# Router products of tile 1 moved ahead of the place counts, and expert 0's rows gathered already transposed

## The chip, the cores and the metric

The kernel runs on one core of a Trainium2 chip. The metric is the device time of one execution in microseconds; lower is better. The engines that matter here are TensorE (PE for its matrix products, PEld for its loads of stationary operands), VectorE (DVE), ScalarE (ACT) and the queue of weight transfers, which SyncE (SP) issues.

## What is computed

One transformer layer on 256 tokens of width 1024, in float32: attention of two kinds (MoBA and NSA, 8 heads each), the output projection with its residual, and a mixture of 32 experts with 4 picked for each token. The part around the change is the beginning of the mixture. Cut from the reference:

```python
x = x + jnp.concatenate([o_moba, o_nsa], axis=-1) @ w_out[l]
x = x + moe_ffn(rmsnorm(x, ffn_norm_g[l]), w_router[l], b_router[l], w_up[l], b_up[l], w_down[l], b_down[l])

# moe_ffn(h):
logits = (ht @ w_router + b_router).astype(jnp.float32)
top_val, top_idx = lax.top_k(logits, TOP_K)          # 4 of 32 experts for each token
wts = jax.nn.softmax(top_val, axis=-1)
# for each expert, with the rows of the tokens that picked it:
a = clamped_swiglu(xb @ w_up[e] + b_up[e])           # 1024 -> 2048 -> 1024
y = a @ w_down[e] + b_down[e]                        # 1024 -> 1024
# and the sum over a token's four experts, weighted by wts
```

The weights of one expert are 12 MB (w_up 8 MB, w_down 4 MB), so 32 experts bring some 400 MB through the transfer queue.

## The kernel before

The 256 tokens are two tiles (0 and 1) of 128 tokens, one token on each partition: `xt[:, n, :]` holds tile n with its 1024 columns. After attention the kernel does the following, in program order on TensorE (lines 1282 to 1315).

- **Projection and turned tiles.** `project` (L1028) multiplies the attention output by w_out, VectorE adds the residual into `xt` (`add_piece`, L1573), and `turn_x2` transposes 128x128 blocks of `xt` (L914) into PSUM, from where ScalarE copies them to `x2T` (`read_x2T`, L789). Tile 1 is turned in three steps: blocks 0 to 3, blocks 4 and 5, blocks 6 and 7.
- **Router.** `route` (L1108) sums eight products of a block of `x2T` (stationary, 128x128) with 32 router columns. Each float32 product shows as two loads and two products in the trace; a transpose shows as one.
- **Top 4.** `top_of(n)` on VectorE (L1579 to L1585) adds the bias, finds the four largest logits of each token of tile n and marks them in `M[:, n, :]`. L1297, L1298 and L1308 are products of a triangle and of ones with `M`, which count the tokens ahead, so that `place_of` (L1591) knows each token's place in each expert's list. `pick_tile(n)` (L1595) makes `pm[:, n, :]`, 128 tokens by 64 places, with the token's 1/rms where it takes that place.
- **Gather of an expert.** `gather_tile(n)` (L1118) multiplies `pm[:, n, :]` (stationary, 128x64) by the 1024 columns of `xt` in two halves of 512, into bank XG of PSUM, and sums over the two tiles. The result lies as places by columns, so ScalarE copies it to `xg` (`read_xg`, L815), `gather_turn` transposes it in four blocks (L1133) into bank XTB, and VectorE multiplies it by the norm's gain into `xgT` (`read_xgT`, L1637). `xgT[:, k, :]` is the stationary operand of the up products.
- **Up, down, combine.** `up` (L1163, 64 loads and 64 products an expert, over blocks k = 0 to 7), preceded by the bias product `up_bias` (L1143); `down` (L1196); `combine` (L1208). `keep_warm` (L1114) issues products whose result nobody reads.
- **Expert 0** has this order of its own: tile 0's `gather_tile` before the counts of tile 1, tile 1's after them, then the bias, the transposes, three warm products, and `up`. ScalarE, between its last copy of `x2T` and `read_xg(0)`, takes the exponential of the top logits (L809) and loads the table for its sigmoid (L810).

The order on every engine is written out by hand; there is no scheduler. The weights arrive in `ring`, ten places of 2 MB, plus `extra`; SyncE issues each transfer when the place has been used. Right around the change it waits first for `logits_done` 2 (the end of tile 1's router products), then for `first_half_used` 1 and 2 (the up products of expert 0 at k = 0 and k = 2), then for `up_used` and `down_used` of the experts that follow.

## Time and profile before

| | |
|---|---|
| median of 3 runs | 1076.32 us |
| lowest and highest of them | 1074.85 and 1077.40 us |
| the profiled execution: its time | 1077.45 us |
| the profiled execution: its span | 1075.4 us |
| mean granted TensorE clock | 0.995 of full |
| TensorE busy | 1031.2 us (96%) |
| VectorE, ScalarE busy | 223.5 us (21%), 155.0 us (14%) |
| transfers | 423.35 MB, mean 394 GB/s |

The span runs from the first to the last instruction of the core; 2.05 us of the profiled execution's time lie outside it. All times of the trace below are in microseconds from the start of the span. TensorE is shown as busy nearly always, but the transfer queue is too, and which of the two is waited for changes along the span, so the share of busy time alone does not tell what an edit is worth.

### The profile page before, as it was taken

Reading aid. Unit: us, or ns where it says so; the run is one execution under the profiler, and the core shown is the slowest. Engines: PE = TensorE matmul, PEld = TensorE weight load, DVE = VectorE, ACT = ScalarE, POOL = GpSimd, SP = SyncE. Lnnn points to the kernel's source line nnn. Section 1 sums busy time; section 2 is a strip of 40 time slices with the busy share of each in tenths; the row PEclk is TensorE's granted clock in tenths of the full one; section 3 lists DMA queues with packets and bytes.
Section 4 is the critical chain, followed back from the end, with each engine's and each line's share of the span. In section 5 each row is a group of like instructions: output and inputs, shape, how many; then the busy total and the mean of one; then the engine's idle time right before and its main releaser. Section 6 shows DMA issues by size and latency. Waiting matters only on the chain.

```text
span 1075.4 us, 12842 instructions
## 1 busy us (share of the span) xinstructions
PE 1031.2 (96%) x5122; PEld 411.5 (38%) x5122; DVE 223.5 (21%) x633; ACT 155.0 (14%) x389; POOL 20.0 (2%) x49
## 2 busy tenths in 40 slices
PE   8999999999999999999999999999999999999996
PEld 6776663333333333333333333333333333333332
DVE  3354533111111111111111111111112101111112
ACT  1233431111100110001111111111101100011102
POOL 4011000000000000000000000000000000000000
PEclk8999999999999999999999999999999999999999
DMA  9993378999999999999999999999999999999994
GB/s 283 317 351 129 121 288 356 403 399 428 427 428 431 433 432 433 431 428 430 431 431 433 435 431 430 430 431 431 436 429 433 430 429 427 427 427 427 428 425 193
DMA packets 36972, 423.35 MB, mean 394 GB/s; under 512 B 8242, under 2 KB 12386, under 8 KB 19012
## 3 DMA queue, kind: packets, MB, share of 16 engines
q1 hardware_dynamic: 36688, 422.34, 94.1%
q8 instruction: 32, 0.52, 0.2%
q10 hardware_dynamic: 244, 0.42, 0.1%
q14 instruction: 8, 0.07, 0.0%
HBM read 421.70 MB, written 1.05 MB: 393 GB/s over the span
## 4 chain that ended last, share of the span: by engine, by line
PE 77%; DMA 19%; DVE 3%; ACT 1%; issue 0%; DVEq 0%; ACTq 0%; SPq 0%
PE ps L1163 31%; DMA ring<-in_w_up_dram 18%; PE ps L1196 17%; PE ps L1208 5%; PE ps L1118 4%; PE ps L941 4%; PE ps L1028 3%; PE ps L948 2%; PE ps L1143 2%; PE ps L979 1%; DVE work L1637 1%; PE ps L1133 1%; DVE work L1681 1%; PE ps L1176 1%; PE ps L1055 1%; PE ps L1067 1%
## 5 line engine op out<-in xcount | busy, mean ns | idle before, releaser
L1163 PE MATMUL ps<-ring,work 128*64 128x512 f32 x2040 | 447.4, 594 | 8.6 <-DMA ring<-in_w_up_dram 8.1
L1163 PEld LDWEIGHTS ps<-ring,work 128*64 128x64 f32 x2040 | 142.7, 137 | 310.3 <-issue 290.7
L1196 PE MATMUL ps<-ring,work 128*64 128x512 f32 x1008 | 223.3, 595 | 21.1 <-DVE work L1681 21.1
L1646 DVE TENSOR_SCALAR work<-ps 128x512 f32<-128x512 f32 x31 | 21.4, 692 | 642.9 <-PE ps L1163 642.9
L1196 PEld LDWEIGHTS ps<-ring,work 128*64 128x64 f32 x1008 | 69.8, 137 | 154.5 <-issue 129.0
L821 ACT ACTIVATE work<-work 128x512 f32<-128x512 f32 x31 | 19.5, 630 | 453.8 <-DVE work L1646 453.8
L1208 PE MATMUL ps<-work 64*128 64x512 f32 x256 | 63.6, 615 | 0.7 <-ACT work L833 0.7
L1118 PE MATMUL ps<-xt,work 128*64 128x512 f32 x256 | 60.6, 593 | 0.2 <-DVE work L1595 0.2
L833 ACT ACTIVATE work<-ps 128x512 f32<-128x512 f32 x32 | 19.1, 597 | 236.5 <-PE ps L1196 236.5
L941 PE MATMUL ps<-extra,ring 128*128 128x256 f32 x192 | 42.7, 380 | 0.0
L1208 PEld LDWEIGHTS ps<-work 64*128 64x128 f32 x256 | 22.0, 186 | 41.8 <-issue 40.2
L941 PEld LDWEIGHTS ps<-extra,ring 128*128 128x128 f32 x192 | 35.9, 190 | 5.0 <-issue 0.4
L1143 PE MATMUL ps<-work 32*64 32x512 f32 x256 | 34.8, 613 | 0.5 <-ACT work L856 0.5
L1637 DVE TENSOR_TENSOR work<-ps,gf_rowsT 128x512 f32<-128x512 f32 x32 | 22.1, 692 | 54.3 <-PE ps L1133 54.3
L1118 PEld LDWEIGHTS ps<-xt,work 128*64 128x64 f32 x256 | 18.2, 137 | 35.8 <-issue 35.4
L1028 PE MATMUL ps<-ring,extra 128*128 128x512 f32 (+1 forms) x72 | 28.7, 546 | 0.0
L948 PE MATMUL ps<-ring,extra 128*128 128x280 f32 (+1 forms) x64 | 22.0, 497 | 0.0
L1649 DVE SCALAR_TENSOR_TENSOR work<-work 128x512 f32<-128x512 f32 x31 | 21.5, 692 | 1.1
L1653 DVE TENSOR_TENSOR work<-work 128x512 f32<-128x512 f32 x31 | 21.5, 692 | 1.1
L1647 DVE TENSOR_SCALAR work<-ps 128x512 f32<-128x512 f32 x31 | 21.1, 681 | 0.0
L815 ACT ACTIVATE work<-ps 128x512 f32<-128x512 f32 x32 | 19.1, 598 | 11.2 <-PE ps L1118 11.2
L828 ACT ACTIVATE work<-ps 128x256 f32<-128x256 f32 x32 | 12.4, 387 | 50.9 <-PE ps L1176 50.9
(254 smaller groups left out, 525.7 us busy)
## 6 DMA issues: line engine op xcount, KB each, us to landing
ring<-in_w_up_dram SPq DMA_DIRECT2D x40, 4096.0 KB, 35.8
ring<-in_w_up_dram SPq DMA_DIRECT2D x43, 2048.0 KB, 18.2
ring<-in_w_down_dram SPq DMA_DIRECT2D x20, 4096.0 KB, 35.9
ring<-in_w_down_dram SPq DMA_DIRECT2D x21, 2048.0 KB, 15.6
ring<-in_w_up_dram SPq DMA_DIRECT2D x9, 1024.0 KB, 13.6
ring<-in_w_in_dram SPq DMA_DIRECT2D x8, 1024.0 KB, 9.4
ring<-in_w_out_dram SPq DMA_DIRECT2D x4, 1024.0 KB, 9.7
ring<-in_w_down_dram SPq DMA_DIRECT2D x4, 1024.0 KB, 30.0
```

The source lines that it names most:

```text
L941: t = pe.matmul(dst, lhs(win_unit(c, k)), normed(k), start=(k == 0), stop=(k == KD - 1))
L948: t = pe.matmul(dst, normed(k)[:, n * P:(n + 1) * P], win_unit(c, k)[:, lo:hi], start=(k == 0), stop=(k == KD - 1))
L1028: t = pe.matmul(dst, oT[:, k, n * P:(n + 1) * P], wout_nsa[:, k, lo:hi] if k < 4 else wout_moba[:, lo // 512, k % 4, lo % 512:lo % 512 + h ...
L1118: t = pe.matmul(ps[h * 64:(h + 1) * 64, XG, :], pm[:, n, :], xt[:, n, h * 512:(h + 1) * 512], start=(n == 0), stop=(n == 1), skip_group_ch ...
L1143: t = pe.matmul(UP[h * 64:h * 64 + 64, a, :], sel[a * E:a * E + E], bup[a * E:a * E + E, :].rearrange("e (p h x) -> e p h x", h=2, x=8)[:, ...
L1163: t = pe.matmul(UP[h * 64:h * 64 + 64, a, :], xgT[:, k, :], row[:, a * 64:(a + 1) * 64, h, :], start=False, stop=(k == KD - 1), skip_group ...
L1196: t = pe.matmul(ps[h * 64:(h + 1) * 64, XG, :], aT[:, j, u * 64:u * 64 + 64], w[:, j * D + h * 512:j * D + (h + 1) * 512], start=(u == 0 a ...
L1208: t = pe.matmul(ps[:, OUT[n][h], :], cT[h * 64:(h + 1) * 64, n, :], yv[h * 64:(h + 1) * 64, :], start=first, stop=True, skip_group_check=True)
L1637: dve.tensor_tensor(xgT.rearrange("p (h j) t -> p j h t", h=2), ps[:, XTB, :].rearrange("p (j h t) -> p j h t", j=4, h=2), gf_rowsT[:].uns ...
L1646: dve.tensor_scalar(t1, up_pairs[:, 0], 7.0, None, ALU.min).then_inc(swi, 1)
L1649: dve.scalar_tensor_tensor(out=t3, in0=t3, scalar=1.0, in1=t1, op0=ALU.add, op1=ALU.mult)\
L1653: dve.tensor_tensor(av, t3, t2, ALU.mult).then_inc(a_ready, 1)
```

## The change

Three things are edited on the way from tile 1's router to expert 0's up products.

1. The first four of tile 1's eight router products are issued before the two count products of tile 0 and the transposes of blocks 6 and 7; before, all eight came behind them.
2. Expert 0's rows are gathered with the operands exchanged: blocks of `xt`, taken with a step of 4 columns, are the stationary operand (128x128), and `pm` (128x64) is the moving one. The result is already transposed, so ScalarE's copy `read_xg(0)` and the four transposes `gather_turn(0)` are gone. There are 16 such products, 8 for each tile. Those of tile 0 are issued behind the router products; those of tile 1 behind `pm_ready`. The halves of the result lie in banks XTB and XG, and VectorE reads each with an operation of its own (`read_first`).
3. `up` of expert 0 waits for the first half of `xgT` alone (`first_xgT`) and for the second only at k = 4. The bias product now stands ahead of the two warm products, the three other warm products are gone, and the later waits on `xg_read` count one less.

```diff
--- before.py
+++ after.py
@@ -315,6 +315,8 @@
         table_done = sem("table_done")
         first_half_used = sem("first_half_used")
         logits_done = sem("logits_done")
+        first_gathered = sem("first_gathered")
+        first_xgT = sem("first_xgT")
         td_ready = sem("td_ready")
         te_ready = sem("te_ready")
         x2T_ready = sem("x2T_ready")
@@ -838,7 +840,6 @@
                 act.activation(sel[0:2 * E], eye2[0:2 * E, ds(e, 1)].broadcast_to([2 * E, TOK]), ACT.Copy)\
                    .then_inc(sel_ready, 1)
 
-            read_xg(0)
             select(1, 1)
             sigmoid(0)
             read_xg(1)
@@ -1113,10 +1114,12 @@
                 for _ in range(n):
                     pe.matmul(ps[:, OUT[0][0], 0:P], ident[:, :], ones[:], start=True, stop=True)
 
-            def gather_tile(n):
-                for h in range(2):
-                    t = pe.matmul(ps[h * 64:(h + 1) * 64, XG, :], pm[:, n, :], xt[:, n, h * 512:(h + 1) * 512],
-                                  start=(n == 0), stop=(n == 1), skip_group_check=True)
+            def first_gather(n, half):
+
+                for j in range(4):
+                    t = pe.matmul(ps[:, (XTB, XG)[half], j * TOK:(j + 1) * TOK],
+                                  xt[:, n, 512 * half + j:512 * half + 512:4], pm[:, n, :],
+                                  start=(n == 0 and j == 0), stop=(n == 1), skip_group_check=True)
                 return t
 
             def gather(b, first=False):
@@ -1124,11 +1127,13 @@
                 if not first:
                     pe.wait_ge(y_read, b - 1)
                 for n in range(NT):
-                    t = gather_tile(n)
+                    for h in range(2):
+                        t = pe.matmul(ps[h * 64:(h + 1) * 64, XG, :], pm[:, n, :], xt[:, n, h * 512:(h + 1) * 512],
+                                      start=(n == 0), stop=(n == 1), skip_group_check=True)
                 t.then_inc(xg_done, 1)
 
             def gather_turn(b):
-                pe.wait_ge(xg_read, b + 1)
+                pe.wait_ge(xg_read, b)
                 for j in range(4):
                     t = pe.transpose(ps[:, XTB, j * P:(j + 1) * P], xg[:, j * P:(j + 1) * P], ident[:, :])
                 t.then_inc(xgT_done, 1)
@@ -1145,18 +1150,22 @@
                                       start=True, stop=False, skip_group_check=True)
                 t.then_inc(bias_used, 1)
 
-            def up(b, prev, unit, biased=False, last=False, halves=False):
-
-                if not biased:
+            def up(b, prev, unit, last=False, first=False):
+
+                if first:
+                    pe.wait_ge(first_xgT, 1)
+                else:
                     up_bias(b, prev)
-                pe.wait_ge(xgT_read, b + 1)
+                    pe.wait_ge(xgT_read, b + 1)
                 for u in range(UP_UNITS):
+                    if first and u == 2:
+                        pe.wait_ge(xgT_read, b + 1)
                     w = unit(u)
                     for j in range(2):
                         k = 2 * u + j
                         if last and k == KD - 1:
                             pe.wait_ge(last_half_in[u], 16)
-                        row = aside if halves and k == 1 else w[:, j * 2 * F:(j + 1) * 2 * F]
+                        row = aside if first and k == 1 else w[:, j * 2 * F:(j + 1) * 2 * F]
                         row = row.rearrange("k (p h x) -> k p h x", h=2, x=8)
                         for a in range(2):
                             for h in range(2):
@@ -1165,13 +1174,13 @@
                                               start=False, stop=(k == KD - 1), skip_group_check=True)
                             if last and k == KD - 1 and a == 0:
                                 t.then_inc(half_up, 1)
-                        if halves and k in (0, 2):
+                        if first and k in (0, 2):
                             t.then_inc(first_half_used, 1)
                     t.then_inc(up_used, 1)
 
             def combine_turn(b, ahead):
                 pe.wait_ge(pw_ready, b + 1)
-                pe.wait_ge(xg_read, b + 1 + ahead)
+                pe.wait_ge(xg_read, b + ahead)
                 for n in range(NT):
                     t = pe.transpose(ps[:, XG, n * P:(n + 1) * P], pw[:, n, :], ident[:, :])
                 t.then_inc(cT_done, 1)
@@ -1292,27 +1301,26 @@
             turn_x2(1, range(0, 4), PJ[0], 3, 1)
             project(ps[:, 6, 0:256], 1, 768, 1024, 4).then_inc(half_done, 1)
             turn_x2(1, range(4, 6), PJ[1], 4, 2)
+            route(1, range(0, 4), 3)
             pe.wait_ge(m_ready, 1)
             pe.wait_ge(const_ready, 7)
             pe.matmul(ps[:, PLACES[0], 0:E], upper[:], M[:, 0, :], start=True, stop=True).then_inc(pos_done, 1)
             pe.matmul(ps[:, PLACES[1], 0:E], ones[:], M[:, 0, :], start=True, stop=False)
             turn_x2(1, range(6, 8), PJ[0], 5, 3)
-            route(1, range(0, 4), 3)
             route(1, range(4, 6), 4)
             route(1, range(6, 8), 5).then_inc(logits_done, 1)
-            pe.wait_ge(bup_in, 32)
-
             pe.wait_ge(pm0_ready, 1)
-            gather_tile(0)
+            first_gather(0, 0)
+            first_gather(0, 1)
             pe.wait_ge(m_ready, 2)
             pe.matmul(ps[:, PLACES[1], 0:E], upper[:], M[:, 1, :], start=False, stop=True).then_inc(pos_done, 1)
+            pe.wait_ge(bup_in, 32)
+            up_bias(0, False)
             keep_warm(2)
             pe.wait_ge(pm_ready, 1)
-            gather_tile(1).then_inc(xg_done, 1)
-            up_bias(0, False)
-            gather_turn(0)
-            keep_warm(3)
-            up(0, False, in_singles(0), biased=True, halves=True)
+            first_gather(1, 0).then_inc(first_gathered, 1)
+            first_gather(1, 1).then_inc(xg_done, 1)
+            up(0, False, in_singles(0), first=True)
             gather(1, first=True)
             combine_turn(0, 1)
             gather_turn(1)
@@ -1632,8 +1640,15 @@
                     t = dve.tensor_scalar(pw[:, n, :], iota_t, place(n), Wt[:, n, ds(e, 1)], ALU.is_equal, ALU.mult)
                 t.then_inc(pw_ready, 1)
 
+            def read_first(half, done, ready):
+
+                dve.wait_ge(done, 1)
+                k = slice(4 * half, 4 * half + 4)
+                dve.tensor_tensor(xgT[:, k, :], ps[:, (XTB, XG)[half], 0:4 * TOK].rearrange("p (k t) -> p k t", k=4),
+                                  gf_rowsT[:, :, half:half + 1].broadcast_to([P, 4, TOK]), ALU.mult).then_inc(ready, 1)
+
             def read_xgT(b):
-                dve.wait_ge(xgT_done, b + 1)
+                dve.wait_ge(xgT_done, b)
                 dve.tensor_tensor(xgT.rearrange("p (h j) t -> p j h t", h=2),
                                   ps[:, XTB, :].rearrange("p (j h t) -> p j h t", j=4, h=2),
                                   gf_rowsT[:].unsqueeze(3).broadcast_to([P, 4, 2, 64]),
@@ -1681,7 +1696,8 @@
                 dve.tensor_copy(aT[:, 2:4, :], UP[:, 1, 0:256].rearrange("p (a q) -> p a q", a=2))\
                    .then_inc(aT_read, 1)
 
-            read_xgT(0)
+            read_first(0, first_gathered, first_xgT)
+            read_first(1, xg_done, xgT_read)
 
             dve.wait_ge(te_ready, 1)
             link(dve.tensor_tensor(texp, texp, M, ALU.mult))
```

On TensorE, from the transposes of blocks 4 and 5 of tile 1 to expert 0's first up products, the program before has these rows (each is line, kind, output<-moving operand,stationary operand, shape of the output, and count; `work` is the tensor in which `pm`, `M`, `xgT` and the router's columns lie, and `extra` holds `x2T`):

```order
L914 MATMUL ps<-ident,xt 128x128 x2
L1297 MATMUL ps<-work,upper 128x32
L1298 MATMUL ps<-work,ones 128x32
L914 MATMUL ps<-ident,xt 128x128 x2
L1108 MATMUL ps<-work,extra 128x32 x8
L1118 MATMUL ps<-xt,work 64x512 x2
L1308 MATMUL ps<-work,upper 128x32
L1114 MATMUL ps<-ones,ident 128x128 x2
L1118 MATMUL ps<-xt,work 64x512 x2
L1143 MATMUL ps<-work 64x512 x4
L1133 MATMUL ps<-ident,work 128x128 x4
L1114 MATMUL ps<-ones,ident 128x128 x3
L1163 MATMUL ps<-ring,work 64x512 x4
```

and the changed program has these (its line numbers are somewhat higher for the same statements; L1109 is `route`, L1120 the new gather, L1148 the bias, L1115 `keep_warm`, L1172 `up`):

```order
L915 MATMUL ps<-ident,xt 128x128 x2
L1109 MATMUL ps<-work,extra 128x32 x4
L1307 MATMUL ps<-work,upper 128x32
L1308 MATMUL ps<-work,ones 128x32
L915 MATMUL ps<-ident,xt 128x128 x2
L1109 MATMUL ps<-work,extra 128x32 x4
L1120 MATMUL ps<-work,xt 128x64 x8
L1316 MATMUL ps<-work,upper 128x32
L1148 MATMUL ps<-work 64x512 x4
L1115 MATMUL ps<-ones,ident 128x128 x2
L1120 MATMUL ps<-work,xt 128x64 x8
L1172 MATMUL ps<-ring,work 64x512 x4
```

Four router products moved ahead of the counts, the gather of 64x512 products became one of 128x64 products, and the four transposes L1133 and three warm products have no successor before `up`.

On VectorE, from tile 1's `pick_tile` to the sums of the softmax (the two rows between them are the difference of the logits and the read of the gathered rows), before:

```order
L1595 TENSOR_SCALAR work<-work,rstd 128x64
L1620 TENSOR_TENSOR work<-work 128x64
L1637 TENSOR_TENSOR work<-ps,gf_rowsT 128x4x2x64
L1687 TENSOR_TENSOR work<-work 128x64
L1688 TENSOR_REDUCE work<-work 128x2
```

and in the changed program, where L1647 is `read_first`:

```order
L1603 TENSOR_SCALAR work<-work,rstd 128x64
L1628 TENSOR_TENSOR work<-work 128x64
L1647 TENSOR_TENSOR work<-ps,gf_rowsT 128x256 x2
L1703 TENSOR_TENSOR work<-work 128x64
L1704 TENSOR_REDUCE work<-work 128x2
```

One read of 128x512 became two of 128x256; what is behind them stands as it did. On ScalarE only the copy L815 of expert 0 between the table load L810 and `select(1, 1)` (L838) is gone.

## Rows read from the trace of the kernel before

**Rows 1.** The page: TensorE and its share; the queue of the weights.
```profile
PE 1031.2 (96%) x5122; PEld 411.5 (38%) x5122; DVE 223.5 (21%) x633; ACT 155.0 (14%) x389; POOL 20.0 (2%) x49
...
q1 hardware_dynamic: 36688, 422.34, 94.1%
```

**Rows 2.** Chain of waits, 620 to 720 us: start, length, what.
```profile
634.02 37.00 DMA ring<-in_w_up_dram
...
691.04 38.26 DMA ring<-in_w_up_dram
```

**Rows 3.** Windows: PE, PEld, DVE, ACT, POOL busy, granted clock, DMA share, GB/s.
```profile
168.00:170.00 2.00, 2.00 (x12) 0.68 (x10) 1.20 (x6) 0.00 (x0) 0.00 (x0) 1.00 0.11 45
170.00:172.00 2.00, 2.00 (x12) 0.72 (x10) 0.00 (x0) 0.00 (x0) 0.00 (x0) 1.00 0.74 242
...
220.00:222.00 2.00, 2.00 (x16) 0.44 (x14) 0.00 (x0) 0.85 (x2) 0.00 (x0) 1.00 0.74 213
222.00:224.00 2.00, 2.00 (x12) 0.68 (x10) 0.00 (x0) 0.00 (x0) 0.00 (x0) 1.00 0.71 270
224.00:240.00 16.00, 16.00 (x79) 5.86 (x76) 2.76 (x5) 1.62 (x3) 0.00 (x0) 1.00 1.01 425
```

**Rows 4.** Timeline of SyncE's queue, 150 to 235 us: start, length, issues.
```profile
169.46 0.33 SPq L483 DMA_DIRECT2D ring<-in_w_down_dram  x1
172.89 2.04 SPq L483 DMA_DIRECT2D ring<-in_w_up_dram  x2
```

**Rows 5.** Chain of waits, 150 to 200 us.
```profile
159.43 1.72 PE ps L1108 x16
...
161.24 0.26 DVE work L1579
...
162.49 0.42 PE ps L1308 x2
...
163.25 0.32 DVE work L1595
...
164.00 1.28 ACT L810
165.29 0.20 ACT root L810
165.50 0.50 ACT work L815
...
166.04 0.67 PE ps L1133 x4
...
166.73 0.70 DVE work L1637
...
167.48 13.95 PE ps L1163 x64
...
192.99 1.02 PE ps L1143 x8
```

**Rows 6.** Timeline of TensorE, 158 to 163 us: start, length, operation.
```profile
158.42 0.30 PEld L1297 LDWEIGHTS ps<-work,upper 128*128 128x128 f32 x2
...
158.99 0.44 PE L914 MATMUL ps<-ident,xt 128*128 128x128 f32 x2
...
159.16 1.86 PEld L1108 LDWEIGHTS ps<-work,extra 128*128 128x128 f32 x16
...
161.06 0.20 PEld L1118 LDWEIGHTS ps<-xt,work 128*64 128x64 f32 x4
...
162.71 0.53 PEld L1114 LDWEIGHTS ps<-ones,ident 128*128 128x128 f32 x4
```

**Rows 7.** Timeline of VectorE and ScalarE, same stretch.
```profile
158.51 0.42 DVE L1573 TENSOR_TENSOR xt<-ps,xt 128x256 f32<-128x256 f32 x1 [0.92 <-PE ps L1028]
...
159.47 0.38 ACT L789 ACTIVATE extra<-ps 128x256 f32<-128x256 f32 x1 [0.35 <-PE ps L914]
```

**Rows 8.** Timeline of stationary loads near the start, two overlapping stretches.
```profile
8.18 0.55 PEld L928 LDWEIGHTS ps<-ident,ring 2*128 2x128 f32 x4
...
8.51 0.21 PEld L928 LDWEIGHTS ps<-ident,ring 2*128 2x128 f32 x1
```

## Prediction

> **What bounds the kernel now.** I read the page first. TensorE is busy for 96% of the span, and the weight queue takes 94% of the transfer engines' time [rows 1]. Two engines so near to full cannot be told apart by their shares, so the next view is the chain of waits. From 634 us on, its long pieces are transfers of w_up of 37 to 38 us [rows 2]: that stretch is bound by the weights, with TensorE's down, gather and up products between as the links that release the next transfer. So an edit near 160 us is worth what it does to the stream of weights, and nothing else.
>
> The windows say where that stream can still be moved. From 224 us on the share is 1.01 at 425 GB/s: it never pauses. Before, it does. Between 168 and 172 us it moves 45 and 242 GB/s, and between 220 and 224 us 213 and 270 GB/s [rows 3]. Against 425 the last pause is worth (1 - 213/425) x 2 + (1 - 270/425) x 2 = 1.7 us. The queue's timeline shows what ends the first: SyncE issues at 169.46 and 172.89 us [rows 4], when the up products of expert 0 have used blocks 0 and 2. So the pauses are waits for TensorE. If TensorE starts `up(0)` earlier by d and then does the same work, each release after it comes earlier by d, the pauses lie earlier, and so does the stream's unbroken part, whose last transfer decides the end. The transfers in flight before 168 us are not moved; the idle time behind them is more than (1 - 45/425) x 2 = 1.8 us [rows 3], so d may be that large before it is cut.
>
> **Where up(0) starts now.** The chain between the router and `up` [rows 5]: router products to 161.15, top 4 on VectorE from 161.24, the count product at 162.49, place and pick to 163.25 + 0.32 = 163.57. Then it turns to ScalarE: a table load of 1.28 us from 164.00 and a small operation at 165.29 stand ahead of the copy `read_xg(0)` (0.50 on the chain, to 166.00), and then come the transposes at 166.04, VectorE's read at 166.73 (0.70) and `up` at 167.48. The gather itself is not on it; it waited for ScalarE's table. The reader should see that all of 163.57 to 167.48, 3.9 us, is this detour.
>
> **The change, step by step.** I follow the time at which TensorE begins a load of stationary operands. The cadence of loads of 128 columns is that of the router: 16 in 1.72 us, 0.1075 us each [rows 5]. Both old and new orders are the same up to 158.42, where the first count product was loaded [rows 6].
>
> 1. *Router order.* Four router products, 8 loads: 0.86, to 159.28. Two count products: one took 0.22 (four loads of 0.1075 for both are 0.43), to 159.72. The transposes of blocks 6 and 7: their loads took 159.16 - 158.99 = 0.17, to 159.89, and their result was there 0.44 after the first load [rows 6], so at 160.16. ScalarE's copy takes 0.38 [rows 7] and starts 0.04 later, 160.58; with the gap of 0.04 to 0.06 that the chain shows between engines, block 6 is usable at 160.64. Meanwhile TensorE does blocks 4 and 5: 4 loads, to 160.32, and waits 0.32. This is a **new wait**: before, the four products now moved away lay between these transposes and the router products that need them. Last 4 loads to 161.07, where before 16 loads from 159.16 [rows 6] ended at 160.88. So logits come **0.19 later**. The stall of VectorE's residual add, which held the transposes at 158.99 (0.12 us beyond the 158.42 + 0.43 of the two products), is absorbed in this. Queued behind the new wait are the last router products and everything after; `logits_done` also releases one half transfer of w_down, but the queue then still has work to 168 us, so 0.19 is hidden there, and would cost 0.19 if it were not.
> 2. *Tile 0's gather.* Before, its first load came 0.18 after the router's last (161.06 against 160.88 [rows 6]); I keep that: 161.25. 8 products of 2 loads at 0.1075 are 1.72, to 162.97. The trace has no load of `xt` by steps of 4 over 128 partitions with 64 moving columns; the moving columns lie between the router's 32 and the transposes' 128, both of which run at about this cadence [rows 5, 6], so I take 0.1075. Under it VectorE's top 4 runs: its chain took 162.49 - 161.24 = 1.25 [rows 5], so from 161.43 the mask is there at 162.68. TensorE comes later, 162.97: the count product is now late because of TensorE, by 0.3.
> 3. *Count, bias, warm products.* Count 0.22 (162.49 to 162.71 [rows 6]), to 163.19. Bias 1.02 (the 8 of L1143 later in the chain [rows 5]), to 164.21. Two warm products, 4 loads, 0.43, to 164.64. VectorE needs from the count's load to the pick 163.57 - 162.49 = 1.08 [rows 5]: 162.97 + 1.08 = 164.05. So the pick is covered by bias and warm products with 0.6 to spare; without them it would cost up to 0.86.
> 4. *Tile 1's gather.* 16 loads, 1.72, to **166.36**. The first half's 8 loads end at 165.50; the last product ends 0.27 after the turn of its load (router: 161.15 against 160.88), so 165.77. VectorE reads 256 columns from PSUM in 0.42 [rows 7], with 0.04 on either side: 166.27. Just before 166.36, so `up` starts when TensorE is free. The second read needs to be done only at k = 4, and `up` takes 13.95 for eight blocks [rows 5], so 7.0 us later: free.
> 5. *Removed.* ScalarE's copy, four transposes and three warm products. ScalarE's exponential and table load are off the path now; `select(1, 1)` and the sigmoid need them only after `up(0)`.
>
> `up(0)` at 166.36 instead of 167.48: **1.1 us earlier**, less than the 1.8 that the first pause can give. Nothing after it is changed. For the profiled execution, 1077.45 us with a span of 1075.4, this gives 1076.3 and 1074.3; it was the slowest of the three, 1.1 above their median. On the median, 1076.32 - 1.1 = **1075.2**.
>
> **Bounds of the unknown price.** Below: if the 32 new loads cost nothing, the count goes out at 162.68, bias and warm products end at 162.68 + 0.22 + 1.02 + 0.43 = 164.35, and the path is then VectorE's, 164.35 + 0.27 + 0.04 + 0.42 + 0.04 = 165.12: gain 2.4. Half the price gives about 1.7. Above: each load longer by x costs 32x; the gain is gone at x = 0.035, a cadence of 0.1425. The nearest row for the step of 4 is L928, which loads `gf_rows` by the same step: 4 loads, the first at 8.18, the last at 8.51, so 0.11 us each [rows 8]. They hold 2 partitions only, but 128 columns as here; so I stay at 0.1075.
>
> The Trainium skill speaks against this change (SBUF — State Buffer, section on the DMA port swizzle): SBUF lines are 16 bytes, and full bandwidth wants at least two hits in a line, though the same passage calls a step of 4 floats free. By its first half every column of this gather opens a line of its own. L928's cadence of 0.11 does not show it; the sum with doubled loads is that of the second rival below.
>
> **Rivals.**
> - *The stream does not follow* (0.14): `up(0)` is earlier, but the end stays, 1076.3. For it: the end is set 900 us later, through transfers of 37 us, and the three runs spread over 2.5 us. Against it: the last pause ends by TensorE's release and is 1.7 us, more than the shift.
> - *Slow stepped loads* (0.08), the other side: each of the 32 loads takes twice as long, 32 x 0.1075 = 3.44 more, `up(0)` at 169.8, 2.3 later than before: 1078.6. It decides from a cadence of 0.1425 for a loss, and from 0.1425 + 2.15/32 = 0.21 for one beyond 0.2%. Against it: L928.
> - *Cheaper loads or better overlap* (0.06): half the price, 1.7 earlier, 1074.6. For it: 64 moving columns need less of the array than 128. Against it: the router's 32 need no less time.
>
> **How the numbers follow.** The forecast has 0.72: 0.8 to 1.3 us faster, since a cadence of 0.117 for 32 loads takes 0.3 back. The range: lowest run less 1.7, 1073.2; highest run with nothing gained, 1077.4, and a little of the slow loads, 1077.6. What a measurement of this kernel can tell from no change is about 0.2%, 2.15 us. The forecast is half of that. A median may be off by 1 us, so beyond 2.15 faster comes from the tail of the forecast and the third rival, 0.14; slower from the second and from spread, 0.06; within, 0.80.
>
> **What would show it.** Right: `up(0)` begins near 166.4 (it has to be within 166.1 to 166.7); a wait of about 0.3 us before the last four router loads, on ScalarE's copy; no wait before the count product of tile 1 nor before tile 1's gather; new loads at 0.11 us; issues of SyncE near 168.3 and 171.8; the last pause of the stream near 219 to 223. Wrong: loads above 0.14 us, a wait of `up` on VectorE of more than 0.2 us, the second half late at k = 4, or a pause of the stream that ends no earlier than before. If all of this holds and the time has moved by more than 2 us, the cause is not this edit's path.

## The result

The changed kernel takes 1082.06 us (median of 4 runs, 1080.59 to 1083.40) against 1075.59 us for the kernel before in the same comparison: ratio 1.0059, 95% interval [1.0047, 1.0071], some 6.3 us slower by the ratio (the two medians lie 6.5 apart). The forecast was 1075.2 us, faster by 1.1. The profiled execution took 1080.59 us, with a span of 1078.6 us.

Line numbers are those of the changed kernel: L1109 is `route`, L1120 the transposed gather, L1316 the count product, L1148 the bias, L1115 the warm products, L1172 `up`. The chain of waits of the changed kernel, 100 to 300 us (start, length, what), to be held against [rows 5]:

```profile
148.83 0.87 PE ps L915 x8
...
157.10 0.39 ACT extra L791
...
157.54 0.63 PE ps L1109 x4
158.17 3.81 PE ps L1120 x16
161.98 0.37 PE ps L1316 x2
162.35 1.91 PE ps L1148 x8
164.27 1.15 PE ps L1115 x4
165.42 3.60 PE ps L1120 x16
169.02 16.10 PE ps L1172 x64
...
197.70 13.88 PE ps L1172 x64
```

Two things are wrong against the forecast. Each gather of 16 loads takes 3.81 and 3.60 us where 1.72 was expected. And from the count product on, everything is slow that the change does not touch: the bias 1.91 instead of 1.02, `up(0)` 16.10 instead of 13.95 [rows 5]. The windows say why (columns as in [rows 3]; the granted clock is the number before the DMA share):

```profile
156.00:158.00 2.00, 1.89 (x18) 1.78 (x18) 1.10 (x6) 0.88 (x3) 0.00 (x0) 1.00 0.85 254
158.00:160.00 2.00, 2.00 (x11) 2.00 (x10) 1.05 (x6) 0.97 (x1) 0.00 (x0) 0.95 1.03 360
160.00:162.00 2.00, 2.00 (x11) 2.00 (x10) 0.00 (x0) 0.00 (x0) 0.00 (x0) 0.50 0.91 324
...
172.00:174.00 2.00, 2.00 (x8) 0.61 (x6) 0.00 (x0) 0.00 (x0) 0.00 (x0) 0.63 0.36 57
174.00:176.00 2.00, 2.00 (x12) 0.61 (x10) 0.00 (x0) 0.00 (x0) 0.00 (x0) 1.00 0.81 332
```

TensorE's clock falls from 2.4 to 1.2 GHz (granted 1.00 to 0.50) during the first transposed gather, with TensorE shown as busy for the full 2.00 us of each window from 158 us on, and comes back some 14 us later, inside `up(0)`. The slow loads are there before the clock falls. Timeline of the stationary loads, 158.6 to 158.9 us, where the granted clock is still 1.00 (it is 1.00 in each half microsecond up to 159.5, and 0.81 in the next):

```profile
158.43 0.80 PEld L1120 LDWEIGHTS ps<-work,xt 128*128 128x128 f32 x3
```

and the loads of the two lines, all together (duration in ns as lowest/median/highest):

```profile
L1120 PEld LDWEIGHTS ps<-work,xt x32: 309/330/333, 158.0 to 168.5; 128*128 128x128 f32 x32
```

```profile
L1109 PEld LDWEIGHTS ps<-work,extra x32: 186/192/192, 151.1 to 157.9; 128*128 128x128 f32 x32
```

Three loads of 0.33 us that together take 0.80 begin (0.80 - 0.33) / 2 = 0.235 us apart; a router load lasts 0.19 and they follow each other by 0.11.

**A yardstick.** Two executions cannot be compared by the clock on the wall alone: TensorE already spends some time at 0.50 near 8 us of the span, more in one execution than in another, and between these profiles this moves all that follows by up to 3.1 us. So I measure from the first transposes of tile 0 (L915 x8, L914 in the kernel before, whose chain has it at 151.97) to the start of `up(1)`. Kernel before: 194.01 - 151.97 = 42.04 us ([rows 5] end at the bias just before it, 192.99 + 1.02). Changed kernel: 197.70 - 148.83 = 48.87, so **6.83 us** later. The spans differ by only 1078.6 - 1075.4 = 3.2 us, because the execution profiled of the kernel before had lost 3.1 at its start; 3.2 + 3.1 is the 6.3 of the ratio. Some 0.5 of the 6.83 therefore does not reach the end.

The record of the clock alone is not enough either. In the profiles of twice and rows_twice_again it shows 1.00 from 8 to 12 us, and yet the eight transposes near 9.8 us take 1.71 us there, as they do at 0.50 in the kernel before, and not the 0.87 that they take in the changed kernel. So where the table below says that the clock stays, it goes by durations too: the bias takes 1.02 us and `up(0)` 13.88 to 13.95 where it stays, 1.91 or 1.92 and 15.37 to 16.10 where it falls.

### The profile page after: what moved, and what is told of

It is laid out like the page before. It is cut to its first block, busy times and chain, and to the rows that moved or that the text cites. A ratio compares the mean times of both kernels' runs of the same rounds, so it can differ in the third digit from the quotient of the medians.

```text
span 1078.6 us, 12845 instructions
## 1 busy us (share of the span) xinstructions
PE 1038.2 (96%) x5136; PEld 418.1 (39%) x5136; DVE 223.7 (21%) x634; ACT 154.3 (14%) x388; POOL 19.9 (2%) x49
## 4 chain that ended last, share of the span: by engine, by line
PE 81%; DMA 15%; DVE 2%; issue 0%; ACT 0%; DVEq 0%; ACTq 0%; SPq 0%
PE ps L1172 34%; PE ps L1205 18%; DMA ring<-in_w_up_dram 14%; PE ps L1217 5%; PE ps L1131 4%; PE ps L942 4%; PE ps L1029 3%; PE ps L1148 2%; PE ps L949 2%; PE ps L980 1%; DVE work L1652 1%; PE ps L1138 1%; DVE work L1696 1%; PE ps L1185 1%; PE ps L1056 1%; PE ps L1120 1%
## 5 line engine op out<-in xcount | busy, mean ns | idle before, releaser
L1172 PE MATMUL ps<-ring,work 128*64 128x512 f32 x2040 | 450.2, 598 | 6.9 <-DMA ring<-in_w_up_dram 6.7
L1172 PEld LDWEIGHTS ps<-ring,work 128*64 128x64 f32 x2040 | 143.3, 138 | 309.9 <-issue 294.2
L1148 PE MATMUL ps<-work 32*64 32x512 f32 x256 | 35.7, 627 | 0.5 <-ACT work L857 0.5
```

The costliest lines, as they stand in the source:

```text
L1148: t = pe.matmul(UP[h * 64:h * 64 + 64, a, :], sel[a * E:a * E + E], bup[a * E:a * E + E, :].rearrange("e (p h x) -> e p h x", h=2, x=8)[:, ...
L1172: t = pe.matmul(UP[h * 64:h * 64 + 64, a, :], xgT[:, k, :], row[:, a * 64:(a + 1) * 64, h, :], start=False, stop=(k == KD - 1), skip_group ...
```

## The experiments

Each kernel is the changed kernel or the kernel before with the edits told in its section. "Local" is the yardstick less 42.04, from the profile of one execution; "ratio" compares 4 to 12 executions with the kernel before in the same session.

| kernel | local, us | clock in its profile | median, us (lowest to highest) | ratio, 95% interval |
|---|---|---|---|---|
| changed | +6.83 | falls | 1082.06 (1080.59 to 1083.40) | 1.0059 [1.0047, 1.0071] |
| contig | -0.84 | stays | 1076.41 (1074.34 to 1080.30) | 1.0002 [0.9989, 1.0016] |
| twice | +3.10 | stays | 1079.20 (1076.50 to 1081.11) | 1.0024 [1.0012, 1.0036] |
| gather_only | +5.93 | falls | 1082.15 (1081.14 to 1083.28) | 1.0048 [1.0031, 1.0066] |
| route_only | +0.17 | stays | 1076.67 (1073.96 to 1078.47) | 1.0003 [0.9991, 1.0015] |
| table_later | -0.40 | stays | 1075.40 (1073.67 to 1077.51) | 0.9992 [0.9982, 1.0003] |
| table_halves | -0.57 | stays | 1075.92 (1073.68 to 1076.49) | 0.9992 [0.9983, 1.0002] |
| table_short | -0.67 | stays | 1075.46 (1073.50 to 1076.95) | 0.9995 [0.9985, 1.0005] |
| rows_best | +3.41 | falls | 1076.50 (1072.90 to 1079.41) | 1.0000 [0.9986, 1.0014] |
| rows_twice | -1.41 | stays | 1074.56 (1073.59 to 1076.39) | 0.9995 [0.9986, 1.0004] |
| rows_twice_again | -1.41 | stays | 1074.73 (1073.44 to 1076.08) | 0.9987 [0.9978, 0.9996] |

### contig: the step taken away

```diff
-                                  xt[:, n, 512 * half + j:512 * half + 512:4], pm[:, n, :],
+                                  xt[:, n, 512 * half + j * P:512 * half + (j + 1) * P], pm[:, n, :],
```

> The changed kernel with expert 0's 16 stationary blocks of xt taken without the step: 128 neighbouring columns in place of every fourth one (expert 0 then multiplies the wrong columns; all instructions keep count and shape). Theory A, the step of 16 bytes makes each load slow and the slow loads starve TensorE until its clock is halved: a load every 0.11 us instead of 0.233, granted clock 1.00 through the gather and up(0), up(0) at about 1.1 us earlier than in the kernel before on the same time base, and 1.1 us faster than before (about 1074.5). Theory B, it is the narrow product (64 moving columns) that is slow: loads stay at 0.23 us, the clock falls to 0.50, and the time stays at about 1082. A mixed outcome (loads at 0.11, clock fallen) would give about 1077 to 1078: up(0) 16.1 instead of 13.95 us.

The profile is as theory A said: the clock stays at 1.00. The stationary loads of this kernel, 160 to 167 us:

```profile
161.12 1.87 PEld L1120 LDWEIGHTS ps<-work,xt 128*128 128x128 f32 x16
162.91 0.30 PEld L1316 LDWEIGHTS ps<-work,upper 128*128 128x128 f32 x2
163.25 0.21 PEld L1148 LDWEIGHTS ps<-work 32*64 32x64 f32 x8
...
164.71 1.87 PEld L1120 LDWEIGHTS ps<-work,xt 128*128 128x128 f32 x16
166.64 0.20 PEld L1172 LDWEIGHTS ps<-ring,work 128*64 128x64 f32 x4
```

Sixteen loads take 1.87 us where the changed kernel's take 3.81 (on the chain the two gathers are 1.81 and 1.73 instead of 3.81 and 3.60), and `up(0)` loads at 166.64 on a base that happens to be the forecast's own (tile 0's transposes at 151.97 in both). The forecast had 166.36. So the working was right for contiguous blocks, and the 64 moving columns are not what is slow: theory B falls. The time is a miss: 1.1 us faster was expected, and the ratio is 1.0002, with an interval from 1.2 us faster to 1.7 slower, which tells a gain of 0.84 neither from nothing nor from a small loss. Two of its ten executions took 1079.43 and 1080.30 us, above the slowest of the kernel before (1077.95), as if those had lost the clock. That is argued: only one execution was profiled. How little one profile says on the clock, steps shows below.

### twice: the step kept, the products made wider

```diff
-                    t = pe.matmul(ps[:, (XTB, XG)[half], j * TOK:(j + 1) * TOK],
-                                  xt[:, n, 512 * half + j:512 * half + 512:4], pm[:, n, :],
+                    t = pe.matmul(ps[:, (XTB, XG)[half], j * P:(j + 1) * P].rearrange("p (a t) -> p a t", a=2),
+                                  xt[:, n, 512 * half + j:512 * half + 512:4],
+                                  pm[:, n, :].unsqueeze(1).broadcast_to([P, 2, TOK]),
...
```

(VectorE's `read_first` then takes the first 64 of each 128 columns.)

> The changed kernel with the step kept, but each new product streams 128 moving columns (pm twice over) instead of 64; the second copy is not read. Theory A1, what lowers the clock is how little the array multiplies under the slow loads: loads stay at 0.233 us, the products hide under them, and the clock stays at 1.00, so only the loads' price is left: 32 x 0.125 = 4.0 less the 1.1 gained, some 2.9 us slower than before, about 1078.5. Theory A2, the clock falls whatever the width of the products under slow loads: 0.50 in the records again and about 1082, or a little more since 128 columns at the low clock take 0.21 us.

Chain of waits:

```profile
160.98 3.81 PE ps L1120 x16
...
164.93 1.02 PE ps L1149 x8
165.95 0.64 PE ps L1115 x4
166.59 3.73 PE ps L1120 x16
170.32 13.88 PE ps L1173 x64
```

The loads are as slow as in the changed kernel, 3.81 and 3.73, but the bias is back at 1.02 and `up(0)` at 13.88: the clock stayed at 1.00. Only the products' width differs, with the places of their results in the bank, and this takes 6.83 - 3.10 = 3.7 us away. What is left, 3.10 local and a ratio of 1.0024 (2.6 us), is A1's 2.9. This is the split: 3.10 + 0.84 = 3.9 us for the loads, 3.7 for the clock, less the 0.84 that the new order saves in contig.

### gather_only and route_only: edit 1 undone, edit 1 alone

```diff
+            route(1, range(0, 4), 3)
             pe.wait_ge(m_ready, 1)
...
             turn_x2(1, range(6, 8), PJ[0], 5, 3)
-            route(1, range(0, 4), 3)
             route(1, range(4, 6), 4)
```

(This is route_only, on the kernel before; gather_only is the reverse edit on the changed kernel.)

> The changed kernel with the router products of tile 1 back behind the count products and the transposes (edit 1 undone, edits 2 and 3 kept). Theory A, edit 1 has no part in the loss: loads at 0.233 us, clock 0.50 through up(0), about 1082 less the 0.2 to 0.4 us of the wait for ScalarE's copy. Rival, edit 1 shifts the lean stretch and causes the fall of the clock: clock 1.00 and about 1078.

> The kernel before with edit 1 alone. Theory A: TensorE waits some 0.3 us for ScalarE's copy of blocks 6 and 7, the logits of tile 1 come 0.2 to 0.3 us later, and so does up(0); clock 1.00; 1075.8, not to be told from before. Rival: the clock falls here too, then up(0) takes 16 us and the time is 2 us or more above before.

gather_only loses the clock too and its time is that of the changed kernel within the noise (5.2 us slower than before by the ratio, 6.3 there): edit 1 is not the cause of the loss. Its local cost is 0.90 lower, more than the 0.2 to 0.4 expected, and the two chains say where: 0.17 is edit 1, up to the end of the router, and 0.73 lies in `up(0)`, which takes 15.37 us instead of 16.10. There the clock fell later, near the end of tile 0's gather (1.00 still from 162 to 164 us, in a gather that began at 161.05), and less of `up(0)` was at 0.50. route_only is 0.17 later, with the new wait for ScalarE's copy plain in its chain, and its time cannot be told from before:

```profile
158.72 0.39 ACT extra L789
159.11 0.04 issue
159.15 0.65 PE ps L1108 x4
```

### steps and loads: how long a load takes, by its step and its partitions

In steps the probes ran at 0.50, so that they could not tell the steps apart:

> Only for the time of a load of stationary operands, by its step and its rows: tile 0's gather uses steps of 1 and 2 floats, tile 1's steps of 3 and 4, and in place of the two warm products stand probes whose result nobody reads (step 4 with 2, 32, 64 and 128 partitions, step 8 with 128, and transposes of 128 partitions with steps 4 and 1). Expert 0's rows are not the right ones. If what counts is how many floats of a 16-byte line are used: steps 1 and 2 at 0.11 us a load, step 4 and 8 at 0.233, step 3 between. If 2 partitions are fast for being few: 0.11 with 2, 0.233 with 128, and something between or one of the two at 32 and 64. If the row L928 was fast for being a transpose: step-4 loads of 2 partitions in a plain product take 0.233, and step-4 transposes of 128 partitions 0.11.

At 0.50 even contiguous blocks are slow (rows_best, below), and the probes of plain products all lay near 0.23 us a load. It took 1086.0 us in its one run. Its tile 0 gather, though, with steps of 1 and 2, ran at 1.00 and at the contiguous pace, in the order of contig; and the clock fell just behind it:

```profile
157.80 1.92 PEld L1120 LDWEIGHTS ps<-work,xt 128*128 128x128 f32 x16
```

```profile
160.00:162.00 2.00, 2.00 (x10) 0.39 (x9) 0.64 (x3) 1.10 (x2) 0.00 (x0) 0.52 0.95 369
```

So steps of 1 and 2 cost alike, and narrow products whose loads are fast can be followed by the fall too. loads (1083.1 us in its one run) puts the probes behind the wide `up` products instead:

```diff
+            def probe(i):
+                t64 = ps[:, XTB, 0:TOK]
+                for _ in range(3 if i < 8 else 4):
+                    if i == 0:
+                        pe.matmul(t64, xt[:, 1, 0:128:1], ones[:, 0:TOK], start=True, stop=True)
...
+                    if i == 3:
+                        pe.matmul(t64, xt[:, 1, 0:512:4], ones[:, 0:TOK], start=True, stop=True)
...
                 up(b, True, unit)
+                if isinstance(b, int) and (2 <= b <= 6 or 25 <= b <= 30):
+                    probe(b - 2 if b <= 6 else b - 20)
```

> Probes at full clock, which the probes of the kernel steps did not have: the kernel before with, behind the up products of experts 2 to 6 and 25 to 30, three or four products each whose result nobody reads. In this order: steps 1, 2, 3, 4, 8 with 128 partitions; step 4 with 2 and with 64 partitions; step 1 with 2 partitions; transposes of 128 partitions with steps 4 and 1; transposes of 2 partitions with step 4. Theory: for products, step 1 at 0.108 us a load and step 4 at 0.233, whatever the partitions; L928 was fast for being a transpose, so transposes with step 4 stay near 0.11. Rival: few partitions make it fast, then step 4 with 2 partitions is at 0.11 in a product too.

Loads of each probe line (ns, lowest/median/highest), in the order of the expectation:

```profile
L1233 PEld LDWEIGHTS ps<-ones,xt x6: 186/192/192, 233.7 to 234.3; 128*128 128x128 f32 x6
L1235 PEld LDWEIGHTS ps<-ones,xt x6: 193/196/197, 262.2 to 262.8; 128*128 128x128 f32 x6
L1237 PEld LDWEIGHTS ps<-ones,xt x6: 252/261/263, 290.8 to 291.6; 128*128 128x128 f32 x6
L1239 PEld LDWEIGHTS ps<-ones,xt x6: 309/330/330, 319.7 to 320.8; 128*128 128x128 f32 x6
L1241 PEld LDWEIGHTS ps<-ones,xt x6: 313/334/336, 348.9 to 350.1; 128*128 128x128 f32 x6
L1243 PEld LDWEIGHTS ps<-ones,xt x6: 302/325/325, 888.4 to 889.5; 2*128 2x128 f32 x6
L1245 PEld LDWEIGHTS ps<-ones,xt x6: 304/327/327, 917.6 to 918.8; 64*128 64x128 f32 x6
L1247 PEld LDWEIGHTS ps<-ones,xt x6: 181/187/187, 946.8 to 947.4; 2*128 2x128 f32 x6
L1249 PEld LDWEIGHTS ps<-ident,xt x4: 198/212/218, 975.3 to 975.7; 128*128 128x128 f32 x4
L1251 PEld LDWEIGHTS ps<-ident,xt x4: 138/141/143, 1003.7 to 1004.0; 128*128 128x128 f32 x4
L1253 PEld LDWEIGHTS ps<-ident,xt x4: 190/212/212, 1032.0 to 1032.3; 2*128 2x128 f32 x4
```

Steps 1 and 2 cost the same (192, 196 ns), step 3 costs 261, steps 4 and 8 cost 330 and 334. The number of partitions does not matter: 325 ns with 2, 327 with 64, 330 with 128. A transpose's load is of a shorter kind: 141 contiguous, 212 with step 4, with 128 partitions and with 2. From its timeline row, step 4 begins a load every (1.48 - 0.33) / 5 = 0.23 us:

```profile
319.67 1.48 PEld L1239 LDWEIGHTS ps<-ones,xt 128*128 128x128 f32 x6 [0.81 <-issue]
```

In pace the transposes pay little for the step: four loads with step 4 take 0.56 us in all and four contiguous ones 0.42, so they begin (0.56 - 0.21) / 3 = 0.12 and (0.42 - 0.14) / 3 = 0.09 us apart. The theory holds and the rival falls: L928 was fast for being a transpose, and not for its 2 partitions.

### table_later, table_halves, table_short: the detour of the kernel before

These take the saving that the change was after from the other side: the gather stays as it was, and ScalarE's table load moves behind its copy (table_later), VectorE reads in halves (table_halves), and the three warm products go (table_short).

```diff
-            act.activation(root[:, 5:6], ident[:, 0:1], ACT.Sigmoid)
...
             read_xg(0)
+            act.activation(root[:, 5:6], ident[:, 0:1], ACT.Sigmoid)
             select(1, 1)
...
```

> The kernel before, with ScalarE's load of the sigmoid table moved from ahead of the copy of expert 0's gathered rows to behind it. If the stretch from 163.57 to 167.48 us was a detour through that table load, the copy starts when the gather ends (164.74 instead of 165.50 on the time base of the kernel before) and up(0) begins 0.7 to 0.8 us earlier, with the clock at 1.00; time 0.7 us lower, too little to be told from no change. If the copy is held by something else, nothing moves.

> The same as table_later, and VectorE reads the turned rows in two halves (blocks 0 to 3 first, 128x256 each), so that up(0) starts on the first: 0.7 to 0.8 and another 0.69 - 0.42 = 0.27 us earlier, about 1.0 us in all on the way to up(0); time about 1.0 us lower.

> table_halves without the three warm products ahead of up(0), which stood last on its chain. up(0) then waits for VectorE's first half: transposes, 0.04, 0.42, 0.04: another 0.4 us earlier, 1.0 in all at up(1); clock 1.00, since the gather's products have 512 columns; time about 1.0 us under before, in one group.

(Shown is table_later; the others add to it what their expectations say.) All three fell short: `up(1)` came 0.40, 0.57 and 0.67 us earlier instead of 0.7, 1.0 and 1.0. Chain of table_later:

```profile
163.24 1.08 PE ps L1118 x4
164.32 1.02 PE ps L1143 x8
165.33 0.60 PE ps L1133 x4
```

With ScalarE out of the way the transposes wait for TensorE's own bias products, which stand ahead of them. Each cover that is taken off shows the next one just beneath. None of the three times can be told from no change.

### rows_best, rows_twice: the idea with contiguous blocks

The step of 4 is there because w_up's rows lie that way in the ring. For expert 0 alone they can be loaded in another order, so that neighbouring columns of x form a block:

```diff
+        first_rows = w_up[0, 0].rearrange("(k p) f -> k p f", p=P)
...
+                if isinstance(e, int) and e == 0:
+                    sp.dma_start(at, first_rows[:, 2 * u + half]).then_inc(loaded, 16)
...
-                                  xt[:, n, 512 * half + j:512 * half + 512:4], pm[:, n, :],
+                                  xt[:, n, 512 * half + j * P:512 * half + (j + 1) * P], pm[:, n, :],
...
-                                  gf_rowsT[:, :, half:half + 1].broadcast_to([P, 4, TOK]), ALU.mult)
+                                  gfT[:, k].unsqueeze(2).broadcast_to([P, 4, TOK]), ALU.mult)
...
-            keep_warm(2)
...
```

> The transposed gather with contiguous stationary blocks, and right results: the w_up rows of expert 0 alone are loaded in the order k, p (neighbouring columns of x in one block), the norm's gain is taken from the column form, edit 1 is undone, and the two warm products ahead of tile 1's gather are left out. Loads at 0.11 us and clock 1.00: gain 0.84 us as the contiguous variant showed, 0.17 from edit 1, and 0.4 from the warm products as far as the pick is not waited for, together some 1.4 us earlier at up(1) than before; time 1.0 to 1.5 us lower. Rival: without warm products and with narrow products the clock falls to 0.50 somewhere before up(0) ends; then 2 us or more are given back.

The rival came true in the profiled execution. Its windows:

```profile
156.00:158.00 2.00, 2.00 (x19) 2.00 (x20) 0.99 (x6) 1.63 (x4) 0.00 (x0) 1.00 0.80 217
158.00:160.00 2.00, 2.00 (x19) 2.00 (x18) 1.06 (x6) 0.23 (x1) 0.00 (x0) 0.93 1.04 430
160.00:162.00 2.00, 2.00 (x10) 0.40 (x9) 0.64 (x3) 0.93 (x2) 0.00 (x0) 0.50 0.98 414
```

and its loads, the second gather at the low clock:

```profile
157.84 1.87 PEld L1126 LDWEIGHTS ps<-work,xt 128*128 128x128 f32 x16
...
162.07 3.49 PEld L1126 LDWEIGHTS ps<-work,xt 128*128 128x128 f32 x16 [1.61 <-issue]
```

The fall does not need slow loads, as in steps. Before it came the router's 16 narrow products and the gather's 16, all at 0.11 us a load. Nor is it the missing warm products: the clock falls before their place (0.93 over 158 to 160 us, with the bias starting at 160.23). Six of its twelve times lie between 1072.90 and 1075.92, six between 1077.09 and 1079.41. The mean clock over the whole span is 0.990 to 0.995 in the upper six and 0.993 to 0.996 in the lower six; that points to a lost clock in the upper ones, but the start of the span counts in it too, so it settles nothing.

rows_twice adds the 128 moving columns of the experiment twice to rows_best:

> rows_best, but each product of the transposed gather streams 128 moving columns (pm twice over, the second copy unread) instead of 64. With contiguous blocks a load takes 0.11 us and 128 columns take 0.107, so this costs nothing, and the array multiplies all the time. If what drops the clock is how little the array multiplies, no execution loses it: times in one group, within 1073 to 1076 as the lower half of rows_best, median about 1074.7, 1.0 to 1.5 us under before. If the clock falls for another reason (the missing warm products, the gap of the top 4), the times lie again in two groups up to 1079.

> The kernel rows_twice once more, for its interval alone. If its up(1) really starts 1.4 us earlier and the stream follows, the median is again 1.0 to 1.5 us under before, with no execution above the slowest of before; if the first result was luck, the ratio comes out at 1.000.

```profile
160.96 1.87 PE ps L1126 x16
162.82 0.14 PE ps L1323 x2
162.97 1.02 PE ps L1155 x8
163.99 1.98 PE ps L1126 x16
165.97 13.88 PE ps L1179 x64
```

The chain of the second profile: no wait between router and `up(0)`, clock at 1.00, 1.41 us earlier at `up(1)` in both profiles, and 22 executions between 1073.44 and 1076.39, none above. The first ratio, 0.9995 [0.9986, 1.0004], is 0.5 us faster and left it open; the second, 0.9987 [0.9978, 0.9996], is 1.4 us faster. No other kernel here is clear of the kernel before on the fast side, and this one is so by the second interval alone, with the 1.41 us of both profiles beside it.

## Why the prediction was wrong, step by step

- **What bounds the kernel: right.** The end followed the start of `up(1)`: 6.83 local gave 6.3 in time and 3.10 gave 2.6; the last pause of the stream, at 220 to 224 us before [rows 3], lies at 224 to 228 us in the changed kernel (172 and 360 GB/s), with `up(1)` 3.7 us later in the span. So the rival that the stream does not follow falls for a later start. For an earlier one it rests on less: -1.41 gave -1.4 in one comparison and -0.5 in the other, and -0.84 (contig) gave +0.2, with an interval that holds both.
- **Step 1, the new wait: right.** 0.32 forecast, 0.22 in the profile: loads stop at 157.32 and go on at 157.54, when ScalarE's copy is done. Edit 1 alone costs 0.17 (0.19 forecast). (The stall of 0.12 named there is 158.99 - 158.85 = 0.14; nothing rests on it.)
- **Step 2, the price of a load: this failed.** "I take 0.1075", drawn from the router's contiguous loads; it was 0.235. My only row with the step, L928 at 0.11 [rows 8], misled: it is a transpose, whose contiguous load lasts 141 ns and not 192, and I compared its pace with that of products. Against its own kind (L914) its 0.21 us was half as long again, and that was to be read in the trace of before. The row also stands where the granted clock is 0.50 (8.10 to 8.50 us), which the prediction does not say; that is not what misled, since the same four loads take 0.55 us at 1.00 in the changed kernel too. The partitions, which I named as the doubt about it, were not the point. The passage of the Trainium skill that I set aside (SBUF — State Buffer, section on the DMA port swizzle) is borne out in the half that asks for two hits in a 16-byte line, steps 1 and 2 against 4 and 8; the other half, that a step of 4 floats is free, is not.
- **The second rival had the loads nearly right:** it said 3.44 us more for the 32 loads and `up(0)` 2.3 later. In twice, where the clock stays, the two gathers take 3.81 + 3.73 - 3.44 = 4.1 more, `up(1)` comes 3.10 later and the time is 2.6 longer. I gave it 0.08, and its 1078.6 us is still 3.5 short of the measured time: it too has no term for the clock.
- **The clock: missing altogether.** No term of the sum, no rival and no sign of being wrong was the clock, and the change leaves TensorE less idle than before (busy 1.46, 1.71 and 1.84 of each 2.00 us from 162 to 168 us before, 2.00 after). The fall came with TensorE busy throughout, and costs: bias 1.91 - 1.02, warm products 1.15 - 0.43, count 0.37 - 0.22, `up(0)` 16.10 - 13.95, together 3.9. With the gathers' (3.81 - 1.72) + (3.60 - 1.72) = 4.0 and the 1.1 forecast this gives 6.8, the local difference.
- **Steps 3 to 5 hold for contiguous loads:** contig starts `up(0)` at 166.64 for 166.36, a gain of 0.84 for 1.12; the count took 0.34 instead of 0.22 and the second gather 1.93 instead of 1.72. The pick was covered, the second half was never waited for.
- **The detour through ScalarE:** the trace had it on the path, but the whole 0.76 between the gather's end and the copy was not to be had (table_later, 0.40), since the bias came next. The prediction called all 3.9 us from 163.57 to 167.48 this detour; most of it is other work, which lay under ScalarE's (the gather and the bias) or has to come behind it (the transposes and VectorE's read).

Open: what makes the clock fall. In the profiles, each gather with 64 moving columns but one was followed by the fall (changed, gather_only, rows_best and steps; not contig, whose order up to the bias steps shares), and none with 128 or 512 was. So the width has been shown to matter with the slow loads (twice against the changed kernel); with fast ones it rests on rows_best against rows_twice, and why one execution of a kernel would keep the clock and another lose it is not known. One execution of each kernel was profiled, so that the upper half of its times are executions that lost the clock is argued and not shown.

## What to carry to other kernels

Price an operation from a row of its own kind: a product by products, a transpose by transposes, and a new step of the stationary operand as an unknown until a probe shows it. When an edit trades few wide products for many narrow ones, ask for the clock of what comes after, since here the 14 us of `up(0)` lost more than half of what the gather itself did. Look at the spread too: rows_best has the lowest single time of all and no gain in its median.

## What the hardware showed that I had not expected

- Stationary loads of 128 columns in float32 products at full clock: 192 ns with step 1, 196 with 2, 261 with 3, 330 with 4, 334 with 8, whether 2 or 128 partitions are loaded.
- The granted clock went from 1.00 to 0.50 with TensorE shown as busy for all of the time, after narrow products (32 and 64 moving columns), in four of the five kernels profiled with them; contig kept 1.00. The same loads with 128 moving columns kept the full pace in every profile taken (twice, rows_twice, rows_twice_again: bias 1.02, `up(0)` 13.88).
- At 1.2 GHz contiguous loads slow down as well (16 in 3.49 us instead of 1.87), and on the chain the second gather takes as long as with the step of 4 (3.61 in rows_best, 3.60 and 3.61 in the changed kernel and gather_only): at the low clock the step costs nothing more there.
- The record of the granted clock can miss a low stretch: 1.00 from 8 to 12 us in the profiles of twice and rows_twice_again, with eight transposes in 1.71 us instead of 0.87.
